# A conditioned hybrid decoder trunk: first conditioning in four column groups, with weight units of the first pass between them

## The reference

```
cond = silu(c)
ada = cond @ w_ada[l] + b_ada[l]          # 2048 -> 12288: six vectors of 2048
sh_m, sc_m, g_m, sh_f, sc_f, g_f = split(ada, 6)
h = x * (1 + sc_m) + sh_m
y = hybrid_mixer(h, ...)                  # h @ w_in[l] (2048 x 6672), three head groups, @ w_out[l] (2048 x 2048)
x = layer_norm(ALPHA * x + (1 + g_m) * y)
h = x * (1 + sc_f) + sh_f
y = square(relu(h @ w1[l])) @ w2[l]       # 2048 x 8192, 8192 x 2048
x = layer_norm(ALPHA * x + (1 + g_f) * y)
```

## Time and profile before

| | us |
|---|---|
| median of 3 runs | 2500.45 (2500.33 to 2501.64) |
| profiled execution, its own time | 2503.25 |
| its span in the trace | 2501.4 |
| TensorE busy | 2397.1 (96%) |
| VectorE busy | 1936.2 (77%) |
| ScalarE busy | 1158.6 (46%) |
| GpSimd busy | 174.0 (7%) |

### The profile page before, as it was taken

The page is one execution under the profiler, slowest core; times in us unless marked ns, Lnnn a source line. Parts: engine busy times, 40 slices in busy tenths (PEclk is TensorE's granted clock), DMA queues, the critical chain, the costliest instruction groups (busy, mean ns, idle before and its releaser), DMA issues.

```text
span 2501.4 us, 32892 instructions
## 1 busy us (share of the span) xinstructions
PE 2397.1 (96%) x13077; PEld 2075.4 (83%) x13077; DVE 1936.2 (77%) x2130; ACT 1158.6 (46%) x1504; POOL 174.0 (7%) x120
## 2 busy tenths in 40 slices
PE   2599999999999999999999999999999999999998
PEld 2599988888888888888879998888888888888886
DVE  7889897888898888889886578778789565655657
ACT  0264475545534434434436446655543443443442
POOL 0002100010011011011010120001001101101001
PEclk9999999999999999999999999999999999999999
DMA  9998477877898898998866536678788655656653
GB/s 387 392 339 297 144 268 240 306 278 265 291 339 312 290 346 304 317 315 313 298 202 177 155 118 194 227 260 286 252 285 303 187 191 191 190 187 193 186 193 118
DMA packets 205053, 633.78 MB, mean 253 GB/s; under 512 B 20236, under 2 KB 20964, under 8 KB 203620
## 3 DMA queue, kind: packets, MB, share of 16 engines
q1 hardware_dynamic: 200320, 614.80, 72.2%
q0 software_dynamic: 3008, 16.32, 1.7%
q10 hardware_dynamic: 1572, 0.56, 0.1%
HBM read 629.50 MB, written 2.10 MB: 252 GB/s over the span
## 4 chain that ended last, share of the span: by engine, by line
PE 90%; DVE 6%; issue 1%; DMA 1%; ACT 1%; SPq 0%; DVEq 0%; ACTq 0%
PE PS L1658 46%; PE PS L1684 17%; PE PS L1686 8%; PE PS L1626 8%; PE PS L1667 4%; PE PS L1640 2%; DVE ACC L1082 2%; DMA RAW<-in_w_ada 1%; DVE WL L1091 1%; PE PS L1715 1%; PE PS L1558 1%; PE PS L1591 1%; DVE CV L1298 0%; DVE ACC L985 0%; PE PS L1847 0%
## 5 line engine op out<-in xcount | busy, mean ns | idle before, releaser
L1091 DVE TENSOR_TENSOR WL<-RAW,WH 128x1024 fp32r<-128x1024 f32 (+1 forms) x800 | 993.8, 1248 | 446.4 <-ACT WH L686 445.4
L686 ACT ACTIVATE WH<-RAW 128x1024 fp32r<-128x1024 f32 (+1 forms) x800 | 831.8, 1044 | 1082.0 <-PE PS L1658 555.1
L1684 PE MATMUL PS<-HT,WH 128*128 128x512 f32 x1792 | 632.5, 398 | 0.0
L1686 PE MATMUL PS<-HT,WL 128*128 128x256 f32 x1792 | 502.5, 280 | 0.0
L1684 PEld LDWEIGHTS PS<-HT,WH 128*128 128x128 f32 x1792 | 336.5, 188 | 82.3 <-issue 0.5
L985 DVE SCALAR_TENSOR_TENSOR ACC<-ADR,CT,ACC 128x1024 f32<-128x1024 f32 x300 | 392.1, 1307 | 11.7 <-DMA ADR<-in_w_ada 9.8
L1658 PE MATMUL PS<-WH,T2h 128*128 128x512 f32 x1208 | 374.2, 391 | 0.0
L1658 PE MATMUL PS<-WL,T2h 128*128 128x512 f32 x1208 | 372.2, 389 | 0.0
L1658 PE MATMUL PS<-WH,T2l 128*128 128x512 f32 x1208 | 371.9, 389 | 0.0
L1686 PEld LDWEIGHTS PS<-HT,WL 128*128 128x128 f32 x1792 | 338.4, 189 | 0.7 <-issue 0.5
L1658 PE MATMUL PS<-WH,HT 128*128 128x512 f32 x1024 | 289.8, 396 | 0.0
(11 more groups left out here) (297 smaller groups left out, 2046.2 us busy)
## 6 DMA issues: line engine op xcount, KB each, us to landing
RAW<-in_w SPq DMA_DIRECT2D x512, 512.0 KB, 4.0
ADR<-in_w_ada SPq DMA_DIRECT2D x320, 512.0 KB, 5.5
RAW<-in_w_in SPq DMA_DIRECT2D x192, 512.0 KB, 3.8
RAW<-in_w_ada SPq DMA_DIRECT2D x64, 512.0 KB, 15.8
RAW<-in_w_out SPq DMA_DIRECT2D x64, 512.0 KB, 5.0
RAW<-in_w_in SPq DMA_DIRECT2D x32, 264.0 KB, 2.6
GB<-in_b_ada POOLq DMA_DIRECT2D x8, 512.0 KB, 7.6
LNG<-in_ln_g POOLq DMA_DIRECT2D x4, 1024.0 KB, 7.7
```

Source lines behind the costliest of these rows:

```text
L686: act.activation(WH[:, wh_slot(layer, n), 0:w], RAW[:, k, 0:w], ACT.Copy).then_inc(hi_done.sem, 1)
L1091: tt(WL[:, k, 0:w], RAW[:, k, 0:w], WH[:, wh_slot(layer, n), 0:w].bitcast(F32), ALU.subtract).then_inc(lo_done.sem, 1)
L1684: mm(bank(p, j)[:, :], WH[:, wh, cols], HT[:, kt, :, :], start=kt == 0, stop=False, skip_group_check=True)
L1686: ins = mm(bank(p, j)[:, SEQ:2 * SEQ], WL[:, wl, cols], HTh[:, kt, :], start=False, stop=kt == KT - 1, skip_group_check=True)
```

## The change

It touches layer 0's first conditioning, the plan of the later ones and the place of the masks.

- The four groups are cut another way: group 0 is the shift and group 1 the scale of columns 0 to 1023; group 2 is shift and scale of columns 1024 to 1535 and group 3 of columns 1536 to 2047. A block of groups 2 and 3 is read as two runs of 512 columns a row.
- 19 of the 64 blocks (BY_TENSOR) are multiplied on TensorE: 8 matmuls of one column, with the block as the stationary operand, straight into the group's PSUM bank (first_block). The other 45 stay on VectorE, now in one chain a group (first_mul). The sum over the partitions adds to the same bank (first_sums).
- SyncE loads units 0 to 11 of pass 0 between the blocks (UNITS_AFTER). The first 48 blocks use 16 slots as before, the last 16 only the seven RAW2 slots.
- Units 0 to 10 of pass 0 run ahead of the last sum (early_unit), their high and low halves between the multiply-adds. The columns are given to ScalarE in three parts (first_cols); 14 units have their halves made in the prologue (PRO_SPLITS).
- ADA_PLAN of layer 0: group 6 from units 0 to 18 to units 12 to 28, and so on to group 5, from units 107 to 134 to units 126 to 140; groups 10 and later keep their places. Layer 1 is unchanged.
- hg_mask stands at the head of the loop step, ahead of lo_split. The constants' load waits for high half 16, the cast of LM moves from (0, 12) to (1, 9), and LMs lies elsewhere.

```diff
+PRO_ROUNDS = 3
+PRO_UNITS, PRO_SPLITS = 11, 14
+BY_TENSOR = [a for a in range(64) if (a < 48 and a % 16 in (3, 6, 9, 12, 15)) or a in (51, 55, 59, 63)]
+BY_VECTOR = [a for a in range(64) if a not in BY_TENSOR]
+UNITS_AFTER = {39: (0,), 41: (1,), 43: (2,), 45: (3,), 49: (4,), 51: (5,), 53: (6,), 55: (7,), 57: (8,), 59: (9,),
+               61: (10,), 63: (11,)}
...
-ADA_PLAN = [[(6, 0, 18), (7, 19, 34), (8, 35, 50), (9, 75, 92), (4, 93, 106), (5, 107, 134),
+ADA_PLAN = [[(6, 12, 28), (7, 29, 50), (8, 75, 92), (9, 93, 106), (4, 107, 125), (5, 126, 140),
...
-        PACC = [[ACC, W("ACC2", 24, [P, UW])], [W("ACC3", 28, [P, UW]), W("ACC4", 4, [P, UW])]]
+        PACC = [ACC, W("ACC2", 24, [P, UW])]
...
+        def pro_used(a):
+
+            if a in BY_TENSOR:
+                return pro_pe.sem, BY_TENSOR.index(a) + 1
+            return ada_mac.sem, 2 + BY_VECTOR.index(a) + 1
+
+        def pro_before(a):
+
+            if a >= PRO_ROUNDS * PRO_SLOTS:
+                return a - (PRO_SLOTS - RAW_SLOTS)
+            return a - PRO_SLOTS
...
-                    sp.wait_ge(ada_mac.sem, 2 + 64 - PRO_SLOTS + n + 1)
+                    sp.wait_ge(*pro_used((PRO_ROUNDS - 1) * PRO_SLOTS + n))
...
             for a in range(64):
                 if a >= PRO_SLOTS:
-                    sp.wait_ge(ada_mac.sem, a - PRO_SLOTS + 3)
+                    sp.wait_ge(*pro_used(pro_before(a)))
+                src = w_ada_r[(a % 16) * P:(a % 16 + 1) * P, 0:2 * D]
+                if a < 32:
+                    src = src[:, a // 16 * D:a // 16 * D + UW]
+                else:
+                    dst = dst.rearrange("p (t n) -> p t n", t=2)
+                    src = src.rearrange("p (t n) -> p t n", t=2)[:, :, UW + (a // 16 - 2) * 512:UW + (a // 16 - 1) * 512]
+                sp.dma_start(dst, src).then_inc(arrived, 16)
+                for n in UNITS_AFTER.get(a, ()):
+                    raw_load(0, n, w_in_r[n * P:(n + 1) * P, COL0[0]:COL0[0] + UW])
...
-            pool.wait_ge(ada_mac.sem, 64 + 2)
+            pool.wait_ge(hi_done.sem, hi_done.at(0, 16))
...
-                if b == 0:
+                if layer == 0 and s == 0 and b in (0, 4):
+                    act.wait_ge(pro_cols.sem, 1 + b // 4)
+                elif b == (6 if layer == 0 and s == 0 else 0):
                     act.wait_ge(cols_set.sem, cols_set.at(layer, s + 1))
...
-            for n in range(2):
+            for b in range(4):
+                h_tiles(0, 0, b)
+            for n in range(PRO_SPLITS):
                 hi_split(0, n)
-            h_tiles(0, 0, 0)
-            for n in range(2, W_SLOTS):
-                hi_split(0, n)
+                if n in (6, 7):
+                    h_tiles(0, 0, n - 2)
+            h_tiles(0, 0, 6)
...
-                        if p == 0 and kt % 2 == 0 and kt < 14:
+                        if layer and p == 0 and kt % 2 == 0 and kt < 14:
                             h_tiles(layer, 0, kt // 2 + 1)
+                        if layer == 0 and at == (0, 10):
+                            h_tiles(0, 0, 7)
...
-                chains = 2 if a < 48 else 1
-                acc, k = PACC[a // 16 % 2][a % chains], a % 16
-                dve.wait_ge(arrived, 16 * (a // PRO_SLOTS + 1))
-                if k < chains:
-                    if a >= 32:
-                        dve.wait_ge(ada_sum.sem, a // 16 - 1)
...
+            def first_mul(a):
+
+                block_, arrived, count = pro_slot(a)
+                acc, k = PACC[a // 16 % 2], a % 16
+                dve.wait_ge(arrived, count)
+                if k == 0:
+                    if a >= 32:
+                        dve.wait_ge(ada_sum.sem, a // 16 - 1)
+                    ins = ts(acc[:, :], block_, CT[:, 0:1], None, ALU.mult)
+                else:
+                    dve.wait_ge(ada_mac.sem, 2 + BY_VECTOR.index(a))
+                    ins = stt(acc[:, :], block_, CT[:, k:k + 1], acc[:, :], ALU.mult, ALU.add)
+                ins.then_inc(ada_mac.sem, 1)
+
+            def first_muls(blocks):
+
+                for a in blocks:
+                    if a in BY_VECTOR:
+                        first_mul(a)
...
+            def first_out(g):
+
+                if g < 2:
+                    ada_out(g + 1, 16 * g, pro_bank(g))
+                    return
+                dve.wait_ge(ada_sum.sem, g + 1)
+                c0 = 8 + 4 * (g - 2)
+                both = slice(c0, c0 + 32)
+                out, bias = (x[:, both].rearrange("p (t n) -> p t n", t=2)[:, :, 0:4] for x in (ADA, PT))
+                tt(out, pro_bank(g)[:, 0:8].rearrange("p (t n) -> p t n", t=2), bias, ALU.add).then_inc(ada_cols.sem, 1)
+
+            def first_cols(g, t0, t1):
+
+                dve.wait_ge(ada_cols.sem, g + 1)
+                ts(SC[:, 0, t0:t1], ADA[:, 16 + t0:16 + t1], 1.0, None, ALU.add)
+                dve.tensor_copy(SH[:, 0, t0:t1], ADA[:, t0:t1]).then_inc((cols_set if g == 3 else pro_cols).sem, 1)
+
+            first_muls(range(0, 16))
+            dve.wait_ge(pro_pt.sem, 1)
+            tables()
...
+            first_cols(1, 0, 8)
+            first_muls(range(36, 39))
+            h_lo(0, 0, 0)
+            first_muls(range(39, 40))
+            h_lo(0, 0, 1)
+            first_muls(range(40, 42))
             lo_split(0, 0)
-            ada_out(4, 24, PB[3])
-            sub_layer_cols(0, 0)
-            for n in range(1, 4):
+            h_lo(0, 0, 2)
+            first_muls(range(42, 43))
+            lo_split(0, 1)
+            h_lo(0, 0, 3)
+            first_muls(range(43, 45))
+            lo_split(0, 2)
+            first_muls(range(45, 46))
+            lo_split(0, 3)
+            first_muls(range(46, 50))
+            lo_split(0, 4)
+            first_out(2)
+            first_cols(2, 8, 12)
+            first_muls(range(50, 52))
+            lo_split(0, 5)
+            first_muls(range(52, 54))
+            lo_split(0, 6)
+            h_lo(0, 0, 4)
+            first_muls(range(54, 56))
+            lo_split(0, 7)
+            h_lo(0, 0, 5)
+            for n in range(8, 12):
+                first_muls(range(40 + 2 * n, 42 + 2 * n))
                 lo_split(0, n)
-            h_lo(0, 0, 0)
-            for n in range(4, W_SLOTS):
-                lo_split(0, n)
+            lo_split(0, 12)
+            first_out(3)
+            first_cols(3, 12, 16)
+            lo_split(0, 13)
+            h_lo(0, 0, 6)
             for layer in range(DEPTH):
                 for p in range(FF0):
                     for kt in range(KT):
                         n = p * KT + kt
                         at = (p, kt)
-                        if (layer or n + AHEAD >= W_SLOTS) and n + AHEAD < FF0 * KT + 2:
+                        if p in (2, 3) and kt in HG_M:
+                            hg_mask(layer, (p - 2) * 4 + HG_M.index(kt), p)
+                        if (layer or n + AHEAD >= PRO_SPLITS) and n + AHEAD < FF0 * KT + 2:
...
-                        if at == (0, 12) and layer == 0:
+                        if at == (1, 9) and layer == 0:
                             dve.wait_ge(pro_k.sem, 16 * 3)
                             dve.tensor_copy(LM[:, :], LMs[:, :]).then_inc(pro_lm.sem, 1)
...
                                ALU.mult).then_inc(hg_eq.sem, 1)
-                        if p in (2, 3) and kt in HG_M:
-                            hg_mask(layer, (p - 2) * 4 + HG_M.index(kt), p)
...
+            def first_block(a):
+
+                g, k = divmod(a, 16)
+                block_, arrived, count = pro_slot(a)
+                pe.wait_ge(arrived, count)
+                for i in range(8):
+                    ins = mm(pro_bank(g)[:, i:i + 1], block_[:, i * P:(i + 1) * P], CT[:, k:k + 1],
+                             start=a % 16 == 3 and i == 0, stop=False, skip_group_check=True)
+                ins.then_inc(pro_pe.sem, 1)
+
+            def first_sums(g):
+
+                pe.wait_ge(*pro_used(BY_VECTOR[-1] if g == 3 else 16 * g + 14))
+                for i in range(8):
+                    ins = mm(pro_bank(g)[:, i:i + 1], PACC[g % 2][:, i * P:(i + 1) * P], ones, start=False,
+                             stop=True, skip_group_check=True)
+                ins.then_inc(ada_sum.sem, 1)
+
+            def early_unit(n):
+
+                first_unit(0, 0, n, 0, n, n == 0, False)
+
+            pe.wait_ge(pro_in.sem, 16 * 6)
+            pe.wait_ge(*pro_used(BY_VECTOR[0]))
+            for a in (3, 6, 9):
+                first_block(a)
+            for b in range(3):
+                x_transpose(0, 0, b)
+            first_block(12)
+            first_block(15)
+            first_sums(0)
+            for a in (19, 22, 25, 28, 31):
+                first_block(a)
+            first_sums(1)
+            first_block(35)
+            first_block(38)
+            pe.wait_ge(ada_cols.sem, 2)
+            x_transpose(0, 0, 3)
+            early_unit(0)
+            first_block(41)
+            x_transpose(0, 0, 4)
+            early_unit(1)
+            first_block(44)
```

(51 more changed lines are left out.)

89 lines of the change are left out of this document (30 added, 59 removed).

## The result

The kernel after the change takes 2516.36 us (median of 5 runs, 2511.63 to 2520.36), the kernel before 2500.33 in the same comparison (5 runs): ratio 1.0065, interval 1.0054 to 1.0076. It is slower; the forecast was 2481.5, with 2494 as the upper end. The profiled execution after took 2512.68 us (span 2510.9), against 2503.25 and 2501.4 before.

The account below looks back on a forecast made before the run. The prediction took DMA and VectorE to bound the first conditioning with TensorE idle, and TensorE to bound everything after. Its terms, -24 - 6 + 11 = -19 us, gave 2481.5 us, own range 2475 to 2488, overall range 2466 to 2494.

Parts of the forecast that it names:

- Part 1: Layer 0's first conditioning: units of pass 0 run between the blocks, unit 11 starts at 116 instead of 140.0, 24 us gained.
- the walk: Program-order timing of the interleaved stage: waits for a sum and low halves; unit 10, block 63 and last sum end at 113.4.
- The clock in this stage: Units 0 to 10: one or two falls of TensorE's clock behind longer waits, 2.6 us allowed.
- The rival of half clock all through: Units 0 to 10 all at half clock, unit 11 starts at 150.2, time 2515.5 us; chance 0.05.
- Part 2: Masks ahead of low halves and thinner conditioning in passes 2 and 3: 6 us gained, 7.7 at best, nothing at worst.
- Part 3: Later plan, units 107 to 140: VectorE's denser multiply-adds stall TensorE at the gate's sum and last_units, 11 us lost (0 to 14).
- The rival of the absorbed burst: Units 126 to 140: the plan's burst of multiply-adds is absorbed, costing 3 instead of 11, time 2473.5 us; chance 0.19.

Follow-up runs that it names:

- seven blocks: Changed kernel with 7 blocks on TensorE, all before unit 0, and group 8 in units 51 to 66: 2489.52 us, ratio 0.9955.
- 19, 13, 7 and 0 blocks: Blocks on TensorE: 19 is the change, 2516.36 us; 13 with its plan, 2501.20; 7 and 0 with group 8 in units 51 to 66, 2489.52 and 2492.17.
- The run with the sums apart: Changed kernel with block 47 ahead of unit 3 and block 63 ahead of unit 10: 2510.48 us, ratio 1.0033.
- the masks alone: Kernel before with only hg_mask moved ahead of lo_split: 2497.06 us, ratio 0.9990.
- the plan alone: Kernel before with only layer 0's ADA_PLAN replaced by that of the change: 2517.76 us, ratio 1.0068.
- the group thinned to 8 columns: Seven blocks on TensorE, group 8 in units 51 to 66, its multiply-adds on 8 of 1024 columns, so not the whole function: 2477.44 us, ratio 0.9911.
- the gap plan: Changed kernel with group 8 in units 51 to 66, then 9, 4 and 5 placed as before the change: 2509.46 us, ratio 1.0031.
- none on TensorE: Changed kernel with all 64 blocks on VectorE and group 8 in units 51 to 66: 2492.17 us, ratio 0.9962.
- 7 with the change's plan: Changed kernel with seven blocks on TensorE and the plan of the change as it is: 2492.60 us, ratio 0.9971.

## Why the prediction was wrong

**Part 1, the step that failed**: "A block on TensorE is 8 weight loads with one column each: 3.57 us for 16 of them is 1.8 us a block", and 0.85 amid units. The row was the column sum of one group, 8 matmuls in 16 records; an f32 matmul of this shape leaves two records. I took the 16 records for two sums, and so priced a block at half. Measured: 3.4 us at half clock, 1.7 amid units; a sum 3.55 and 1.8 (2.6 where the clock fell in it).
- Before unit 0 this turned TensorE, "little to do", into the engine that bounds. Blocks, sums and transposes came to 51.35 us, from 26.35 on, and unit 0, 4.2 us behind them, to 81.93: 13.7 us late. It also held back the loads, since the slots of its blocks came free late.
- From unit 0 to unit 11 I had 116 - 68.2 = 47.8 us, and it took 54.0. Seven blocks at 0.86 us more are 6.0. The two sums, priced by the same mistake, and the dearer falls of the clock add to it; the waits that the walk had did not come, as TensorE was busy all through. So 13.7 + 6.2 = 19.9, from 116 to 135.9.
- The mechanism itself was right. With seven blocks, unit 0 starts at 70.2, unit 11 at 115.2 and pass 1 25.1 us earlier (24 forecast), VectorE bounding as in the walk and the DMA engines full. The runs with 19, 13, 7 and 0 blocks put the failure on the price.

**The clock in this stage.** One or two falls, 2.6 us, was right in number (clock 0.57 around 105 us, 0.76 around 137), too low in price (by that column 3.4 and 1.7 us) and wrong in cause: I looked for them behind waits, and they stood behind 32 column records in a row. The run with the sums apart has neither. The rival of half clock all through did not happen: outside those stretches 8 of the units' matmuls took 1.12 us from the second unit on.

**Part 2, 6 us forecast**: about 6 us were gained, in part by luck. Passes 1 to 3 gained 3.8 us (160.8 for 164.7): the masks alone give 1.4 there and the plan alone 2.4. From the last HGRN2 to the last Mamba output came 1.6 more: the fall of the clock at 380.6 us is absent, and the forecast had nothing on it. Behind the layer norm 0.4. The falls of clock behind the masks: in layer 0 seven traces with the masks ahead (after among them) have a wait of 1.5 to 1.6 us for the masked scores instead of 1.98, and none has a fall behind it. In layer 1 all twelve traces with the masks ahead have the same wait of 2.0 us; seven of them have the fall behind it, five (after among them) have not. So that fall depends on the execution, and its going is not the change's work.

**Part 3, 11 us forecast, 18.3 measured**, above the range of 0 to 14. The mechanism was right in place and in clock time: last multiply-add to end at 563.1, ended at 562.7; gate out to be done at 566.7 to 568, done at 567.95. The rival of the absorbed burst did not come, with the interleave or without it (8.10 and 7.93 us of wait). What was mis-sized:
- TensorE came to the sum at 554.8, not 558.3, since the earlier parts had moved it; VectorE started group 5 at 516.76 and took 46.0 us where I had 43.0, 2.5 of them waits for blocks. So it waited 8.10 us, not 4.8.
- The gate's sum itself ran at half clock, 3.75 us, then came the gate out: 1.54 more. TensorE spent 5.2 us on the two gate sums of this stage where it had spent 2.6 before: half clock cost 2.5 us there where I took 1.7. (The clock of 0.67 in 560 to 570 counts idle time too.)
- Three waits ahead of group 5 (0.66, 2.15, 1.67) I had not at all: group 4 was denser than what had stood in units 107 to 125 (group 5 took 28 units before). The plan alone shows them too; that the density makes them is argued, not shown.
- By these rows 4.5 + 8.1 + 1.5 + 2.5 = 16.6 of the 18.3. Another 0.8 is a column sum that now falls into this stage, and 0.9 is not placed.

**The sum.** By the profile: -3.0 (to pass 1), -5.4 (to the last Mamba output), +18.3, -0.4: +9.5. The forecast had -24, -6, +11. The rest of the 16 us of the medians is where the two profiled executions lie among their runs, and why is open. The other four executions after took 2511.63 to 2520.36, and only one is in the trace; their mean granted clock (0.983 to 0.989, 0.992 in the profiled one) does not order them by time.

**What I had not seen at all** couples Parts 1 and 3. Units 0 to 18 were freed of group 6 to leave VectorE time for the early units (no run here keeps group 6 there, so that it is needed is not shown), and its multiply-adds have to go somewhere behind: by the plans, 15 of them stood in pass 0 before and 4 after. The last column of the table prices that, whatever the place: 430.4 to 435.4 us in all eleven runs that carry them whole behind the first 12 units (the run of after, and ten experiments), 419.1 before, 419.4 with the group thinned to 8 columns. The place only decides where TensorE waits: 18.3 us in passes 7 and 8, 15.3 beside the masks, 21.5 in passes 1 to 3. The plan alone, with the masks where they were, adds 434.9 - 419.1 = 15.8 us. The full group against the thinned one, all else alike, is 433.0 - 419.4 = 13.6 us for 16 multiply-adds of 1.2. VectorE's busy time from pass 1 to the layer norm agrees: 358.6 us before (155 to 574), 372.2 with seven blocks and the gap plan (130 to 563). So of the 25.1 us that the interleaving gives by pass 1, some 14 are paid back behind it. My sum set the 24 against a loss of 11 that I took for a fault of one burst; it was the price of the move itself.

The lowest time of a whole kernel here is that of 7 blocks and the gap plan: 2489.52 us, ratio 0.9955. The intervals of none on TensorE and of 7 with the change's plan overlap with its.

## What to carry to other kernels

Before pricing an operation by a row, count its records against the loop in the code: two records for each matmul, taken for two matmuls, halved every price here. Work moved to a second engine must be summed on that engine over the whole stage, at its clock there; 19 blocks made the helper the bound, and 7 brought pass 1 3.8 us earlier than none, little of which was left at the end. When a schedule is pushed back, price the place where the displaced work ends up first: the plan alone cost as much as the whole change did.

## What the runs showed of the hardware

- A 128x128 f32 stationary operand with one moving column leaves two records, 0.213 us each at half clock (17.07 us from start to start for 80) and 0.107 at full (1.71 us from start to start for 16). The Trainium skill (TensorE: Matmul & The Clock Gate, LDWEIGHTS) prices a weight load in ns by its columns over 1.2; for 128 columns that is an estimate of 0.107 us. The records at full clock agree; at half clock they take twice that.
- From 26.35 to 77.7 us TensorE was busy all the time, mostly with one-column matmuls, and kept the rate of half clock (0.213 us a record). The clock's column tells nothing there, as its records begin at 85.4 us. The units' matmuls of 256 columns that follow (2.07 us for 8 at 81.93) were at full rate from 85.5 us on.
- 32 one-column records in a row amid units (3.6 us and more) had the clock fall in or right behind them at all ten places in five traces. 16 in a row at full rate had a fall behind them at 3 of some 70 places, all three at the sum of unit 92. In the run with the sums apart both falls went.
- Waits of 2.5 us for masked scores were followed by a clock of 0.59 in the 4 us behind: 1.6 us on top of the wait. A wait of 2.0 us in layer 1 was followed by a fall in seven of twelve traces.
